# PEER: the gated one-hot rows move from VectorE to GpSimd, and one group of four tokens is spread per key

## The reference

```python
def peer_mixer(h, w_q, keys_1, keys_2, u_tab, v_tab):
    ...
    e1 = jnp.take_along_axis(i1, ci // PEER_TOPK, axis=-1)
    e2 = jnp.take_along_axis(i2, ci % PEER_TOPK, axis=-1)
    experts = (e1 * PEER_N_KEYS + e2).reshape(t, PEER_HEADS * PEER_TOPK)
    gates = jax.nn.softmax(sc, axis=-1).reshape(t, PEER_HEADS * PEER_TOPK)
    def expert_block(args):
        hb, eb, gb = args
        a = jax.nn.gelu(jnp.einsum('td,ted->te', hb, u_tab[eb]).astype(jnp.float32), approximate=False)
        w = (gb * a).astype(hb.dtype)
        return jnp.einsum('te,ted->td', w, v_tab[eb])
```

## Time and profile before

| | |
|---|---|
| median of 3 runs | 2742.7 us (2741.93 to 2743.73) |
| the profiled execution | 2743.37 us, its span 2741.6 us |
| mean granted TensorE clock | 0.930 |
| PE busy | 2447.4 us (89%) |
| DVE busy | 1155.4 us (42%) |
| ACT busy | 702.8 us (26%) |
| POOL busy | 22.6 us (1%) |

### The profile page before, as it was taken

The page is one execution under the profiler, slowest core; times in us unless marked ns, Lnnn a source line. Parts: engine busy times, 40 slices in busy tenths (PEclk is TensorE's granted clock), DMA queues, the critical chain, the costliest instruction groups (busy, mean ns, idle before and its releaser), DMA issues. The chain is left out here.

```text
span 2741.6 us, 34189 instructions
## 1 busy us (share of the span) xinstructions
PE 2447.4 (89%) x13841; PEld 1622.2 (59%) x13841; DVE 1155.4 (42%) x2363; ACT 702.8 (26%) x1213; POOL 22.6 (1%) x36
## 2 busy tenths in 40 slices
PE   8998999968998888988888875679999999999997
PEld 6786677853222222222222263568999889888886
DVE  4647872130100110100011124327887775588886
ACT  2125563010000000000000012223454444455444
POOL 1000000000000000000000000000000000000000
PEclk8999999967999999899999887599999999999999
DMA  4374446515999999999999922021775445678774
GB/s 149 118 220 154 155 154 207 181 44 228 427 428 428 428 427 428 427 428 428 428 427 428 417 87 92 1 77 39 230 228 164 141 140 192 221 241 242 243 243 139
DMA packets 204940, 677.01 MB, mean 247 GB/s; under 512 B 14976, under 2 KB 137104, under 8 KB 180240
## 3 DMA queue, kind: packets, MB, share of 16 engines
q1 hardware_dynamic: 204512, 675.15, 66.4%
q10 hardware_dynamic: 304, 0.15, 0.0%
HBM read 657.40 MB, written 17.83 MB: 246 GB/s over the span
## 5 line engine op out<-in xcount | busy, mean ns | idle before, releaser
L1094 PE MATMUL ps<-ring,tokens 128*34 128x512 f32 x1536 | 371.1, 636 | 39.5 <-DMA ring<-in_w_up 20.3
L574 PE MATMUL ps<-u,ring 128*128 128x272 f32 x1280 | 307.7, 398 | 1.1 <-DVE u L536 1.1
L1094 PEld LDWEIGHTS ps<-ring,tokens 128*34 128x34 f32 x1536 | 90.6, 119 | 313.2 <-issue 244.9
L574 PEld LDWEIGHTS ps<-u,ring 128*128 128x128 f32 x1280 | 242.5, 192 | 54.0 <-issue 4.4
L1693 PE MATMUL ps<-m_hi,row_hi 128*128 128x256 f32 x1024 | 255.3, 287 | 1.8 <-ACT row_hi L1766 1.8
L1693 PE MATMUL ps<-m_lo,row_hi 128*128 128x256 f32 x1024 | 250.7, 283 | 0.0
L1147 DVE TENSOR_TENSOR hidden<-silu,ps 98x512 f32<-98x512 f32 x32 | 21.8, 682 | 497.1 <-PE ps L1094 497.1
L1693 PEld LDWEIGHTS ps<-m_hi,row_hi 128*128 128x128 f32 x1024 | 195.9, 191 | 2.6 <-issue 1.9
L1693 PEld LDWEIGHTS ps<-m_lo,row_hi 128*128 128x128 f32 x1024 | 196.2, 192 | 0.0
L1552 DVE TENSOR_TENSOR row_lo<-u,row_hi 128x1024 fp32r<-128x1024 f32 x128 | 156.7, 1224 | 73.5 <-ACT row_hi L1766 73.1
L1552 DVE TENSOR_TENSOR row_lo<-rows,row_hi 128x1024 fp32r<-128x1024 f32 x128 | 156.4, 1224 | 62.8 <-ACT row_hi L1766 62.2
(11 more groups left out here) (351 smaller groups left out, 3073.1 us busy)
## 6 DMA issues: line engine op xcount, KB each, us to landing
ring<-in_w_gate SPq DMA_DIRECT2D x48, 2048.0 KB, 24.5
ring<-in_w_up SPq DMA_DIRECT2D x48, 2048.0 KB, 25.7
extra_early<-in_w_down SPq DMA_DIRECT2D x32, 2048.0 KB, 21.4
ring<-in_w_down SPq DMA_DIRECT2D x32, 2048.0 KB, 24.4
ring<-in_w_in SPq DMA_DIRECT2D x36, 1024.0 KB, 5.4
extra_early<-in_w_gate SPq DMA_DIRECT2D x16, 2048.0 KB, 24.7
extra_early<-in_w_up SPq DMA_DIRECT2D x16, 2048.0 KB, 25.7
rows<-in_peer_u SPq DMA_DIRECT2D x64, 512.0 KB, 3.7
```

The costliest lines, as they stand in the source:

```text
L574: last = pe.matmul(bank[:, 0:T], wt[:, k, c:c + P], src[:, k, :], start=k == 0, stop=k == kt - 1)
L1094: last = pe.matmul(s.ps[HALF * j:HALF * j + CAP, 2 * c + u % 2, :], s.tokens[:, 2 * (u // 2) + k, :], rows[:, k, 1024 * c + 512 * j:1024 * ...
```

## The change

GpSimd gets a program in the PEER part: it waits for the transposed lists and then makes the four h1 row blocks of each of the 64 groups, in order, with the same `tensor_scalar` as DVE did, and signals a new semaphore `hot_gate`. DVE makes only h2. PE waits for both. A group now takes 1.0 of the room and a key adds 1.0, which puts one group on each of the keys 56 to 119, and none on keys 120 to 127.

```diff
-SPREAD_A_KEY = 2.0
+SPREAD_A_KEY = 1.0
@@ hot_work, DVE
-                    h1, h2 = hot_buffers(g)
+                    h2 = hot_buffers(g)[1]
                     at = slice(TOKENS * g, TOKENS * g + TOKENS)
-                    for t in range(TOKENS):
-                        k = TOKENS * g + t
-                        dve.tensor_scalar(h1[:, t, :], s.iota[:, 0:KEYS], e1[:, k:k + 1], gate[:, k:k + 1],
-                                          ALU.is_equal, ALU.mult)
                     dve.tensor_tensor(h2, s.iota[:, 0:KEYS].unsqueeze(1).to_broadcast([P, TOKENS, KEYS]),
                                       e2[:, at].unsqueeze(2).to_broadcast([P, TOKENS, KEYS]), ALU.is_equal)\
                        .then_inc(hot, 1)
                     pace.hot.append(pace.key)
-                    yield 1.5
+                    yield 1.0
@@ new
+        @block.gpsimd
+        def _(pool):
+            pool.wait_ge(turned_out, BATCHES * QT)
+            for g in range(groups):
+                if g >= 2:
+                    pool.wait_ge(product, g - 1)
+                h1 = hot_buffers(g)[0]
+                for t in range(TOKENS):
+                    k = TOKENS * g + t
+                    last = pool.tensor_scalar(h1[:, t, :], s.iota[:, 0:KEYS], e1[:, k:k + 1], gate[:, k:k + 1],
+                                              ALU.is_equal, ALU.mult)
+                last.then_inc(hot_gate, 1)
@@ spread_weights, PE
                 pe.wait_ge(hot, g + 1)
+                pe.wait_ge(hot_gate, g + 1)
```

More of the change, by code:

```diff
@@ L1528, in peer @@
     names = ("query", "query_out", "scores", "scores_out", "shifted", "exp", "lists", "turned", "turned_out", "m2_hi",
-             "m2_lo", "hi", "lo", "hidden", "gelu", "hot", "product", "spread", "weighted", "act_hi", "act_lo", "used", "y")
+             "m2_lo", "hi", "lo", "hidden", "gelu", "hot", "hot_gate", "product", "spread", "weighted", "act_hi", "act_lo", "used", "y")
     (query, query_out, scores, scores_out, shifted, exped, lists, turned, turned_out, m2_hi, m2_lo, hi_done, lo_done, hidden,
-     gelu, hot, product, spread, weighted, act_hi, act_lo, used, y_out) = (s.sem(f"peer_{k}") for k in names)
+     gelu, hot, hot_gate, product, spread, weighted, act_hi, act_lo, used, y_out) = (s.sem(f"peer_{k}") for k in names)
     row_in = [s.sem(f"peer_row_in{q}") for q in range(ROWS)]
```

## The result

The change makes the kernel slower. The median of 6 runs is 2760.58 us (2758.94 to 2765.59), against 2743.01 us (2741.93 to 2744.91) for 6 runs of the kernel before: a ratio of 1.0066, 95% interval 1.0053 to 1.0079, or 17.6 us (0.7%). The forecast was 2717, with 2745 as the top of the range. Rival B of the prediction happened.

What follows compares the result with a forecast made beforehand. PE was taken as the bound, with some 25.6 us of waits in keys 56 to 103. The profiled 2743.37 us less 25.5 for the pace, other terms at nothing, gave 2717.9, the median 0.7 lower: forecast 2717, range 2713 to 2745.

Steps and rivals of the forecast that it cites:

- Rival B: GpSimd becomes the bound; PE waits for `hot_gate` in keys 56 to 119: 2756 us at X = 0.62; chance 0.19.
- X: Time of one GpSimd `tensor_scalar` of 128x128 with two scalar columns, taken as 0.35 us; four make a group's h1.
- bound of 0.62: Upper bound in us on GpSimd's instruction: a quarter of the 2.47 us 128x512 select.
- hidden behind PE's 3.77 us: GpSimd's group of 1.4 us was to fit within PE's 3.77 us for a key with one group, costing nothing.
- break-even of 0.57: With exclusion, the value of X in us at which the gain is gone and GpSimd decides.
- slower: Outcome of a time above the kernel before, given by Rival B alone: chance 0.19.
- Rival A: GpSimd a little too slow, part of the gain: at X = 0.51 a key takes 3.94 us, 2728 us; chance 0.14.
- Full exclusion: DVE and GpSimd never overlap: 1.90 + 4X us a key, 3.30 at X = 0.35, so cost nothing.
- The pace: One group a key on keys 56 to 119 removes PE's waits: 241.3 us in place of 266.8, -25.5 us.
- `rest` wouldn't be late: `rest` of keys 56 to 119 was to be done 3.7 us before PE needs it.
- the full gain: The forecast outcome, 2717 us with keys 56 to 119 at 3.77 us each; chance 0.63.
- 46 places: Places (31 and 15) in the kernel before where the `row_lo` matmuls were said to wait for DVE's `rest`.

Runs made afterwards that it cites:

- e4: The changed kernel, but GpSimd makes h1 of three of the four tokens and VectorE that of the fourth: 2719.68 us.
- e9: The changed kernel with two numbers in place of the two scalar columns in GpSimd's instruction, both steps kept: 2718.76 us, one run.
- e5: The changed kernel with each of GpSimd's tensor_scalar instructions cut into two of 64 columns: 2841.68 us, one run.
- e6: The changed kernel with GpSimd's second step left out, so no gate and one column of scalars: 2717.55 us, one run.
- e3: The changed kernel with VectorE's `rest` of keys 56 to 119 cut to 8 of 1024 columns: 2717.59 us.
- e7: The changed kernel with VectorE's `rest` of keys 56 to 119 replaced by a tensor_reduce over the same 1024 columns: 2718.97 us.
- e1: The kernel before with the new pace alone, one group a key on keys 56 to 119, all h1 on VectorE: 2718.4 us.
- e2: The changed kernel with the pace of before, so only the move of h1 to GpSimd: 2783.44 us.

## Why the prediction was wrong

The step that failed is the price of GpSimd's instruction: "I add 0.06 for the second step and the scalars and take X = 0.35". It is 0.775 from start to start, more than twice that, and above the bound of 0.62 that I had set from above. So the cost "nothing, hidden behind PE's 3.77 us" was wrong: a group with its hold takes 4.45 us, and PE waits for the rest, 0.68 us a key. By its own break-even of 0.57 with exclusion the prediction gives "slower" for 0.775: the mechanism and its condition stood in rival B, and the size of one term was off.

- **Why X was wrong.** A line through memset, select and copy was taken for the price of any operation with one tensor input. But those have no column of scalars, and one step only. Here 0.17 us went to the columns, the fixed part was 0.335 in place of 0.18, and an element cost 3.4 ns in place of 0.86. The 2.47 us of the 128x512 select was set aside as alone off the line. It was the only row that said GpSimd has operations of more than 4 ns an element, and a quarter of it isn't an upper bound for another operation anyway. The columns are less than half of the miss: with two numbers in their place the instruction still takes 0.60, 0.25 above X, and no run says how that divides between the steps and the rest. Rival A had thought of twice VectorE's 0.26 us; it is three times.
- **The hold was right in kind and dear in size.** Full exclusion had been priced at VectorE's whole 1.90 us a key, the sum of two durations; from h2's start to the end of `rest` it is 1.83. The hold was 1.35 in the changed kernel, and 1.2 to 1.45 in e4, e9, e5 and e6. Two things make it shorter than 1.83. h2 started 0.27 us before the GpSimd instruction then under way had ended (2088.49 and 2088.76), and neither took longer than usual, so the two don't exclude each other for whole instructions. And the held instruction ended 0.57 us after `rest`, so some 0.2 of its 0.775 had been done before. 1.83 - 0.27 - 0.2 is 1.36. With 1.90 the group would have been 5.0 us and the kernel at 2796.
- **It takes both.** Without the hold, 4 x 0.775 = 3.10 us would have been hidden behind PE's 3.77, and e3 and e7 show that with 0.5 us of it left (3.6). With a lower X the hold would have been hidden too, and e6 and e9 show that at 0.58 and 0.60, e6 with nothing to spare.
- **The pace was right.** -25.5 us was forecast for the stretch, and e1's stretch is 25.5 under that of before (241.27 and 266.8). The profiled executions differ by 25.3, the medians of one chip job by 23.8. That `rest` wouldn't be late was right as well: PE waits nowhere for it in the changed kernel, where it takes 1.22 us still.
- **The point that I made and didn't use.** The prediction says that the pace needs no GpSimd and that the move "can only keep that gain or spoil it". It still gave "slower" only 0.19, and the full gain 0.63, on a price for which the trace had no row.
- **A misreading that no term rests on.** The "46 places" in which the `row_lo` matmuls wait count some twice. PEld and PE are the weight load and its matmul, and they wait in the same place: both start at 2088.54. There are at most 31, the number of the weight loads, with 24.1 us in all. The sum goes by the length of the stretch instead.

The faster versions, e1 (2718.4 us) and e4 (2719.68 us), aren't told apart by the runs. In e1's spread stretch PE is busy for all of the 241.27 us, so as long as PE's own list stays as it is, no arrangement of VectorE and GpSimd can shorten it; e1 is the simpler one.

## What to carry to other kernels

When work moves to an idle engine to relieve another, first ask whether the other one is still late once the order has been mended; here a change of pace alone gave the whole gain. Price an operation on GpSimd by a row of the same operation, with its columns and steps, and not by a memset or a copy, and test the sum against the period of the engine that sets the pace. Add to it a hold, here 1.2 to 1.45 us for 1.83 us of VectorE's work with two SBUF inputs, and look for who pays.

## What the runs showed of the hardware

**The hold falls mostly on one side.** GpSimd lost 1.35 us of each group to VectorE. VectorE lost nothing in the changed kernel (h2 0.69, `rest` 1.22), 0.09 us in e4 and e9 (`rest` 1.31), 0.06 in e5 (h2 0.75), and some 0.2 in e2 (h2 0.90 and 0.91 there, in two rows of its timeline). Why it loses so much less was not tried. In the kernel before, a `tensor_scalar` of VectorE took 2.7 us longer than usual while a long memset of GpSimd was under way. If that was the memset's doing, which no run tested, VectorE can be the one that pays.

**The granted clock fell behind PE's longer waits, in e2 alone.** Windows of e2, and the wait of its PE timeline in them:

```profile
2320.00:2324.00 4.00, 3.43 (x28) 3.04 (x26) 1.80 (x3) 1.59 (x3) 4.00 (x5) 1.00 0.36 117
2324.00:2328.00 4.00, 1.59 (x13) 1.62 (x14) 2.15 (x3) 1.03 (x3) 4.00 (x5) 0.97 0.43 145
2328.00:2332.00 4.00, 4.00 (x24) 4.00 (x24) 1.40 (x2) 0.23 (x2) 4.00 (x4) 0.60 0.12 49
2332.00:2336.00 4.00, 4.00 (x37) 4.00 (x36) 1.29 (x1) 2.06 (x5) 1.87 (x3) 1.00 0.50 164
```

```profile
2326.41 1.13 PE L1693 MATMUL ps<-hot 128*128 128x128 f32 x8 [2.76 <-issue]
```

PE had stood for 2.76 us before 2326.41, and some 1.4 us after it began again the clock was at 1.2 GHz: matmuls with `row_hi` started every 0.21 us instead of 0.12. It was back at 2.4 GHz in the next window. The same followed each of e2's nine waits of 2.2 to 2.8 us at L1693, each with a stretch of 4 us at a granted clock of 0.50 to 0.74, and none of its 13 shorter ones (0.8 to 1.4 us). In the changed kernel, whose waits are 0.45 to 0.6 us each, the clock stays at 1.00 throughout the spread (27.1 us in 60 places at L1693; e2 had 38.9 in 22, the longest 2.8). It also stays at 1.00 throughout e5's spread, where PE waits up to 1.7 us in each key. The fall hardly cost e2 any time. GpSimd bounds that stretch, and in all of it GpSimd waited for PE only once, 0.4 us.
